# One head of a gated linear recurrence: score products on two 64-column tiles of TensorE, levels issued in pairs

## The reference, cut to what matters

```
bcum = jnp.cumsum(gc, axis=2)
o_inter = jnp.einsum("bhcd,bhde->bhce", qc * jnp.exp(bcum), state)
diff = bcum[:, :, :, None, :] - bcum[:, :, None, :, :]
decay = jnp.where(causal, jnp.exp(jnp.where(causal, diff, 0.0)), 0.0)
attn = jnp.einsum("bhid,bhijd,bhjd->bhij", qc, decay, kc)
o = o_inter + jnp.einsum("bhij,bhje->bhie", attn, vc)
b_last = bcum[:, :, -1:, :]
state = (jnp.exp(b_last[:, :, 0, :])[..., None] * state
         + jnp.einsum("bhcd,bhce->bhde", kc * jnp.exp(b_last - bcum), vc))
```

## Time and profile before

| | |
|---|---|
| median of three runs | 2506.85 us |
| the profiled execution's own time | 2506.27 us |
| its span, first to last instruction | 2504.5 us |
| mean granted TensorE clock | 0.998 of full speed |
| stretch with the eight heads | about 490 to 960 us of the span |
| one head in the loop, period | 59.37 us (a level at 554.90, 614.27 and 673.65 us in the chain of waits) |

### The profile page before, as it was taken

How to read it: one execution, slowest core, us unless ns; L and a number is a source line. 1 busy time by engine, 2 the same in 40 slices (tenths; PEclk the granted TensorE clock), 3 DMA queues, 4 the chain that set the end, 5 groups by cost and what they waited for, 6 DMA issues and landing times.

```text
span 2504.5 us, 31325 instructions
## 1 busy us (share of the span) xinstructions
PE 2478.6 (99%) x11554; PEld 2057.9 (82%) x11554; DVE 1489.8 (59%) x1647; ACT 584.6 (23%) x790; POOL 1225.7 (49%) x953
## 2 busy tenths in 40 slices
PE   8999999999999999999999999999999999999998
PEld 5788888888888888888888887788778888888887
DVE  6896577688888887699554637652871231622223
ACT  4100444422222222111122214252331110211011
POOL 0433333322232222333567767745776666766664
PEclk9999999999999999999999999999999999999999
DMA  7222122211111112333664445422532233423233
GB/s 273 93 76 81 62 74 68 75 34 50 42 42 47 45 50 101 117 143 109 244 219 150 143 143 160 175 87 78 166 118 93 97 96 98 163 92 101 93 100 118
DMA packets 85973, 270.14 MB, mean 108 GB/s; under 512 B 7952, under 2 KB 11280, under 8 KB 84880
## 3 DMA queue, kind: packets, MB, share of 16 engines
q1 hardware_dynamic: 73936, 246.13, 29.1%
q10 hardware_dynamic: 11968, 23.07, 2.6%
HBM read 224.60 MB, written 44.56 MB: 107 GB/s over the span
## 4 chain that ended last, share of the span: by engine, by line
PE 92%; DVE 2%; POOL 2%; issue 1%; DMA 1%; ACT 1%; SPq 0%; ACTq 0%; POOLq 0%; DVEq 0%
PE ps L393 27%; PE ps L395 27%; PE ps L394 27%; PE xb L534 2%; PE ps L457 1%; POOL w_lo L2052 1%; PE ps L447 1%; DMA w_raw<-wall 1%; POOL w_hi L2050 1%; PE xb L605 1%; PE xb L557 1%; PE xb L560 0%; PE xa L548 0%; PE xb L393 0%; PE xb L395 0%
## 5 line engine op out<-in xcount | busy, mean ns | idle before, releaser
L2052 POOL TENSOR_TENSOR w_lo<-w_raw,w_hi 128x1024 fp32r<-128x1024 f32 x308 | 779.3, 2530 | 25.7
L2049 POOL TENSOR_TENSOR small<-small 128x1 f32<-128x1 f32 x308 | 84.6, 275 | 1190.7 <-PE ps L395 1004.5
L393 PE MATMUL ps<-h_hi,w_hi 128*128 128x512 f32 x1408 | 557.1, 396 | 0.2 <-DVE hg_zc L1152 0.2
L395 PE MATMUL ps<-h_hi,w_lo 128*128 128x512 f32 x1408 | 549.2, 390 | 0.0
L394 PE MATMUL ps<-h_lo,w_hi 128*128 128x512 f32 x1408 | 548.9, 390 | 0.0
L393 PE MATMUL ps<-yb_hi,w_hi 128*128 128x512 f32 x1024 | 402.2, 393 | 2.5 <-POOL w_lo L2052 1.9
L394 PE MATMUL ps<-yb_lo,w_hi 128*128 128x512 f32 x1024 | 398.9, 390 | 0.0
L395 PE MATMUL ps<-yb_hi,w_lo 128*128 128x512 f32 x1024 | 398.9, 390 | 0.0
L2050 POOL TENSOR_SCALAR w_hi<-w_raw 128x1024 fp32r<-128x1024 f32 x308 | 343.7, 1116 | 0.0
L395 PEld LDWEIGHTS ps<-h_hi,w_lo 128*128 128x128 f32 x1408 | 264.3, 188 | 55.4
L393 PEld LDWEIGHTS ps<-h_hi,w_hi 128*128 128x128 f32 x1408 | 264.8, 188 | 53.7 <-issue 1.2
(11 more groups left out here) (287 smaller groups left out, 2938.9 us busy)
## 6 DMA issues: line engine op xcount, KB each, us to landing
w_raw<-wall SPq DMA_DIRECT2D x312, 512.0 KB, 3.5
gst<-gate_d SPq DMA_DIRECT2D x24, 512.0 KB, 4.5
w_kv<-wall SPq DMA_DIRECT2D x16, 512.0 KB, 4.8
x_d<-xx ACTq DMA_DIRECT2D x16, 512.0 KB, 3.1
gate_d<-sigb SPq DMA_DIRECT2D x12, 512.0 KB, 2.6
gate_d<-gbuf SPq DMA_DIRECT2D x12, 512.0 KB, 2.8
xs_xa<-x_d ACTq DMA_DIRECT2D x12, 512.0 KB, 5.2
x_sb<-xT SPq DMA_DIRECT2D x2, 2048.0 KB, 15.6
```

The costliest lines, as they stand in the source:

```text
L393: nc.tensor.matmul(out, wh, xh, start=start, stop=False)
L395: return nc.tensor.matmul(out, wl, xh, start=False, stop=stop)
L2049: nc.gpsimd.tensor_tensor(small[:, 13:14], small[:, 12:13], small[:, 12:13], ALU.add)
L2052: nc.gpsimd.tensor_tensor(w_lo[:, u], w_raw[:, u], w_hi[:, u].bitcast(F32), ALU.subtract).then_inc(w_split, 1)
```

## The change

The score products of the levels and of the diagonal run on two column tiles of the array. `tile_position=(0, side * w)` places a matmul with 64 stationary columns on the left or the right half of the columns, and its result on partitions 0 to 63 or 64 to 127. Each former matmul of a level becomes two with 64 keys each. At levels 1 to 6 a key of the one half of a chunk meets only queries of the same half, so each of the two takes 2x32 queries; at level 7 the left keys meet the first direction's queries and the right keys the second's, 64 each. The diagonal does the same with 64 keys and 64 queries. The blocks that no product writes any more are not read: the mask of the diagonal is applied in two parts of 64 partitions, and head 0 clears `attn` once.

The order on PE changes too. Levels stand in pairs: 1 with 2, 3 with 4, 5 with 6, and 7 alone. Between two pairs stand two quarters instead of one quarter between two levels.

```diff
@@ level(h, l)
+                w = CHUNK // 2
+                bank = xb[:, (l % 2) * HALF:(l % 2 + 1) * HALF]
                 for c in range(NCH // 2):
-                    w = CHUNK // 2
-                    mm = nc.tensor.matmul(pairs(xb, (l % 2) * HALF + c * w, HALF // 2, 1, w, w)[:, :, 0],
-                                          hkp[l % 3][:, c * CHUNK:(c + 1) * CHUNK],
-                                          pairs(hqp[l % 4], c * w, HALF // 2, 1, w, w)[:, :, 0], start=True, stop=True)
+                    for side in range(2):
+                        rows = slice(side * w, (side + 1) * w)
+                        keys = hkp[l % 3][:, c * CHUNK + side * w:c * CHUNK + (side + 1) * w]
+                        if l < LEVELS:
+                            cols = slice(c * w + side * w // 2, c * w + (side + 1) * w // 2)
+                            out_, queries = (x.rearrange("p (s n) -> p s n", s=2)[:, :, cols] for x in (bank[rows], hqp[l % 4][:]))
+                        else:
+                            cols = slice(side * HALF // 2 + c * w, side * HALF // 2 + (c + 1) * w)
+                            out_, queries = bank[rows, cols], hqp[l % 4][:, cols]
+                        mm = nc.tensor.matmul(out_, keys, queries, start=True, stop=True, tile_position=(0, side * w))
                 mm.then_inc(lv_done, 1)
+
+            def diagonal_blocks(c, ch):
+                w = CHUNK // 2
+                for side in range(2):
+                    cols = slice(c * CHUNK + side * w, c * CHUNK + (side + 1) * w)
+                    mm = nc.tensor.matmul(xb[side * w:(side + 1) * w, cols], hg["k"][:, cols], hg["q"][:, cols],
+                                          start=True, stop=True, tile_position=(0, side * w))
+                return mm
@@ tiles_beside_tail(m, h)
                 quarter_of(0, 0, 0)
+                level(h - 1, LEVELS - 2)
                 level(h - 1, LEVELS - 1)
                 quarter_of(0, 0, 1)
+                quarter_of(0, 1, 0)
                 level(h - 1, LEVELS)
-                quarter_of(0, 1, 0)
                 keys_turn(h)
@@ the loop over heads, PE
-                per_chunk(NCH, lambda c, ch: nc.tensor.matmul(
-                    xb[:, ch], hg["k"][:, ch], hg["q"][:, ch], start=True, stop=True)).then_inc(diag_done, 1)
-                if first(h):
-                    take(m + 1, 1)
-                    quarter_of(1, 0, 0)
-                    level(h, 1)
-                else:
+                per_chunk(NCH, diagonal_blocks).then_inc(diag_done, 1)
+                if not first(h):
                     half_of(0, 1).then_inc(mm_done, 1)
-                    level(h, 1)
-                    take(m + 1, 1)
-                    quarter_of(1, 0, 0)
+                take(m + 1, 1)
+                quarter_of(1, 0, 0)
+                level(h, 1)
                 level(h, 2)
                 quarter_of(1, 0, 1)
+                quarter_of(1, 1, 0)
                 level(h, 3)
-                quarter_of(1, 1, 0)
                 level(h, 4)
                 quarter_of(1, 1, 1).then_inc(mm_done, 1)
-                level(h, 5)
@@ head(h), DVE
                 dve.wait_ge(diag_done, h + 1)
-                v.tensor_tensor(hg["attn"][:].rearrange("p (n c) -> p n c", c=CHUNK), xb[:].rearrange("p (n c) -> p n c", c=CHUNK),
-                                ident[:].rearrange("p (o c) -> p o c", o=1).to_broadcast([P, NCH, CHUNK]), ALU.mult).then_inc(lv_free, 1)
+                if first(h):
+                    s.wait(s.at(v.memset(hg["attn"][:], 0.0)))
+                w = CHUNK // 2
+                for side in range(2):
+                    part = slice(side * w, (side + 1) * w)
+                    out_, scores = (x[part, :].rearrange("p (n c) -> p n c", c=CHUNK)[:, :, part] for x in (hg["attn"], xb))
+                    ins = v.tensor_tensor(out_, scores, ident[part, part].rearrange("p (o c) -> p o c", o=1).to_broadcast([w, NCH, w]),
+                                          ALU.mult)
+                ins.then_inc(lv_free, 1)
```

## The result

The changed kernel takes 2519.39 us (median of 5 runs, 2517.51 to 2523.22) against 2506.58 (5 runs, 2505.68 to 2506.98). The ratio is 1.0054, with an interval from 1.0043 to 1.0066. It is 12.8 us slower; I had forecast 7.2 us slower, with a range that holds the measured time. The profiled execution took 2518.97 us, its span is 2517.2 us, 12.7 more than the 2504.5 of before.

What follows compares the result with a forecast made beforehand. PE bounds the kernel, with DVE's chain second. Head 0 at +0.15 us and heads 1 to 7 at +1.0 each make +7.2 on the profiled 2506.3, 2513.5; with 0.6 for the median, 2514 us, range 2498 to 2536.

Steps and rivals of the forecast that it cites:

- What bounds the kernel: Whole kernel: PE, busy 99% of the span, sets the time unless it waits; DVE is second, 79% in the heads.
- The cost of a level, 0.70: Level products on PE: 0.70 us a level for 0.91, the diagonal 1.40 for 1.80, taking 1.85 us from a head.
- A change of tiling, 0.20: PE entering or leaving half-width tiles: 0.20 us each, the weight load exposed; ten changes cost 2.0 us a head.
- DVE's wait for level 1, 2.6: DVE ahead of its copy of level 1: idle 2.6 us in heads 1 to 7, as level 1 comes one quarter later.
- POOL's bursts on DVE's operations: DVE's operations between SBUF tiles take about 2.8 us instead of 0.69 while POOL makes `w_lo`, around 620 and 631.
- The waits of PE, 0.85 at level 4 and none at level 6: PE in heads 1 to 7: waits 0.70 us at level 4 plus 0.15 for an exposed load; no further wait.
- The sum: Head 0 +0.15 us, heads 1 to 7 +1.0 each, together +7.2 us, giving 2514 us; chance 0.45.
- no overlap: Tiles on PE don't overlap: level and diagonal stay at 0.91 and 1.80, +2.2 us a head, 2524; chance 0.22.
- a floor per record: PE's records have a minimum cost whatever their size: up to 1.8 us a level, 80 us in all, 2587; chance 0.05.
- first rival: The same claim as no overlap: PE's tiles don't overlap, +2.2 us a head, 2524 us; chance 0.22.
- the third: DVE's chain holds PE but tiles give it back: waits of 4.2 against a gain of 4.1, 2505 to 2510; chance 0.13.
- The fourth: Tiles run side by side, changes cost 0.1, DVE doesn't hold PE: a head 3.1 us shorter, 2482; chance 0.15.

Runs made afterwards that it cites:

- e8: Kernel e6 with levels 1 to 5 on four tiles of 32 columns instead of two tiles; 2500.34 us, ratio 0.9976.
- e10: Kernel e8 with level 6 moved behind the next quarter, so levels 5, 6 and 7 stand one quarter apart; 2491.12 us, ratio 0.9941.
- e5: Changed kernel with a level's left-tile matmuls all first, then the right tile's, instead of alternating; 2522.45 us (1 run).
- e2: Kernel before with the changed kernel's PE order but products of full width, no tiles; 2521.03 us, ratio 1.0057.
- e9: Changed kernel with POOL making `w_lo` for only half of the blocks through the heads, which leaves work out; 2487.12 us (1 run).
- e6: Kernel e3 with head 0 put back to the changed kernel's order (pair, two quarters, pair); 2491.38 us, ratio 0.9941.
- e3: Changed kernel with levels 1 and 2 as a pair directly behind the half; 2493.34 us, ratio 0.9947.
- e7: Changed kernel without DVE's operation that makes the keys of level 4, whose scores are then wrong; 2518.09 us (1 run).
- e4: Same PE order as e3 but products of full width, no tiles; 2508.23 us, ratio 1.0007 against the kernel before.
- e1: Changed kernel with its tiles kept but PE's order of the kernel before; 2499.93 us, ratio 0.9974.

## Why the prediction was right, and where its sizes were off

**What bounds the kernel**: right. PE's microseconds count as long as PE doesn't wait, and DVE's chain is the second limit (e8 and e10 reach it with a faster PE).

**The cost of a level, 0.70**: too high. It is 0.48, near the lower bound of 0.45. I took the middle because some overlap seemed likelier than full overlap; as long as the tiles alternate it is nearly full (0.030 us from start to start, 0.043 to 0.050 where they don't, e5). The diagonal is 0.96 for 1.40.

**A change of tiling, 0.20**: right within 0.02; it is 0.18. The Trainium skill's rule that a change of mode drains TensorE (TensorEngine Tiling (Array Packing), Key Properties) agrees with what the trace shows, 0.36 us for entry and exit together, 1.8 us in a head. Its other rule, that different tiles load and multiply in parallel, agrees too, and it was worth more. The work of a head on PE alone is thus 4 x 1.31 + 0.84 = 6.08 us for 8.15, 2.1 less, where I had 0.15 more.

**DVE's wait for level 1, 2.6**: 1.76, at the place named, seven times. It is shorter because diagonal and level are done sooner; without the tiles it is 2.66 (e2).

**POOL's bursts on DVE's operations**: right. 2.77 and 2.87 us at 622 and 633, in a head that by its diagonal runs 1.6 us later than the one forecast at 620 and 631. That they lengthen the chain is shown by e9. But the forecast let `widen(3)` start behind the first `w_hi`; it ran beside it and took 1.57 us for 0.69.

**The waits of PE, 0.85 at level 4 and none at level 6**: mis-sized, 1.63 and 1.87 us of lost time. Counted from the head's diagonal, at level 4 the miss is PE's: DVE frees the bank 18.35 us on for 18.7 forecast, and PE, without the wait, would be there at 16.7 for 18.1. At level 6 PE is 0.9 us earlier than forecast, but the larger part is DVE's: the copy of level 4 ends 27.85 us on, for 26.1 forecast. From the end of the copy of level 2 to that of level 4 the forecast had 7.4 us, the trace has 9.5; without a burst the same operations take 6.5 (620.33 to 628.86 before, less 2.06). The second burst costs 3.0 us there, and the forecast left room for 0.9. The prediction had worked this case too: with levels of 0.45 it had waits of 2.0 and 2.2 that eat a gain of 4.1. Measured with the changes in: waits of 3.5 against a gain of 2.1, net 1.4, within its 0.1 to 2.1 a head.

**The sum**: +1.0 a head forecast, +1.41 measured. Another 3.2 us come from the lower clock in two heads, which no step of the prediction had. Of the miss of 5.5 us (12.7 for 7.2) the heads' difference is 7 x 0.41 = 2.9 and the clock 3.2; the half microsecond that is not traced is the rest, with the other sign. That a head came out near the forecast is in part luck: PE's own work was 2.2 us a head cheaper than forecast (-2.07 for +0.15) and the waits 2.65 us longer (3.50 for 0.85). At level 4 the one causes the other; at level 6 the larger part of the wait has a cause of its own.

The rivals: no overlap and a floor per record are refuted by the spacing of 0.030 us. The time alone would not have told: 2519.39 lies as near to the first rival's 2524 as to the forecast's 2514. The waits do take the tiles' whole gain, as in the third, but more than that. The fourth, a head of 57.2 us, is what the same tiles do when level 1 stays behind the half (e6).

What stays open: whether the waits alone bring the clock down. In all eight places in the profiles of the changed kernel, e3, e6 and e7 it falls directly behind a wait of PE, of 1.6 to 1.75 us in seven of them and of 3.16 in e3; but most waits of 1.6 us aren't followed by it, nor are those of 1.82 us in head 0 of e4 and 1.96 in head 0 of e8. No experiment took it apart. The runs of the changed kernel reach from 2517.51 us, at a mean clock of 0.998, to 2523.22 at 0.996; that the number of such stretches makes this spread is likely and not shown.

## What to carry to other kernels

A product that starts another engine's chain goes into the queue of the busy engine as early as it can, and the filling work behind it: the place of one quarter cost 26 us (2519.39 for 2493.34 in e3), and the tiles give 14.9 at best (e4 to e3). A gain on the bound engine counts only up to the slack of the next chain, so read that slack first, and expect that cheaper work there can even be slower (e8). Where two engines slow each other down, ask ahead of which wait the slow stretch falls: in every profile here whose PE waits at level 4 or 6 in the third head, a `w_lo` lies ahead of the copy that frees that bank, and where no wait is left in that head, each `w_lo` starts when its copy is done or nearly done (before, e1, e3, e4, e6). The exception is e10, whose level 6 comes a quarter later. Where an operation's new form is in no row, work the whole chain at both bounds before choosing a value: here the sum hardly hung on it, the waits did.

## What the runs showed of the hardware

- The records of f32 products (two for each, with a load each) start 0.030 us apart with 64 columns on two column tiles that alternate, 0.043 to 0.050 us apart where a tile follows itself (e5), and 0.009 us apart with 32 columns on four tiles (e8). The former ones of 128 columns were 0.112 us apart.
- Entering the tiles and leaving them costs 0.36 us together, among matmuls of 512 columns that start 0.227 us apart.
- Directly behind some of PE's waits of 1.6 to 3.2 us its clock was at 1.2 GHz for about 3.4 us, at a price of 1.6 us each (changed kernel, e3, e6, e7).
- Where DVE's operation on SBUF tiles started 0.02 us behind POOL's `w_hi`, DVE's took 1.57 us for 0.69; where it started 0.10 us ahead, it kept its 0.68 and POOL's took 1.50 for 1.05 (e8 and e6, second burst of the third head).
